# ScalarE's copy of a transposed tile, moved between the side work of two rounds in the fox stage

## What is computed

```python
s = einsum(q, k) * scale + fq[..., None] - cum_logf      # per block of 128 queries
s = where(k_pos <= q_pos, s, NEG_BIG)
p = softmax(s, axis=-1)
out = einsum(p, v)                                        # then a norm per head
# beside it in the same stage, from the other mixers:
y = gelu(y_s5); y = y * sigmoid(y @ w_glu)                # S5's gate
logf = log_sigmoid(z) + log1p(lb * exp(min(-z, 60)))      # HGRN2's gates
k = (1 - lb) * sigmoid(-z)
qk = silu(conv(concat(q, k)))                             # mLSTM's short convolution
```

## Time and profile before

| | us |
|---|---|
| median of 3 runs (1586.54 to 1592.84) | 1587.22 |
| the profiled execution | 1587.83 |
| its span, first to last instruction | 1586.0 |
| TensorE busy in it | 1505.0 (95%) |
| VectorE busy | 817.4 (52%) |
| ScalarE busy | 575.5 (36%) |
| GpSimd busy | 299.1 (19%) |
| the fox stage, 1009.86 to 1075.64 | 65.8 |

### The profile page before, as it was taken

How to read it: one execution, slowest core, us unless ns; L and a number is a source line. 1 busy time by engine, 2 the same in 40 slices (tenths; PEclk the granted TensorE clock), 3 DMA queues, 4 the chain that set the end, 5 groups by cost and what they waited for, 6 DMA issues and landing times. The chain is left out here.

```text
span 1586.0 us, 18617 instructions
## 1 busy us (share of the span) xinstructions
PE 1505.0 (95%) x7560; PEld 1227.5 (77%) x7560; DVE 817.4 (52%) x1137; ACT 575.5 (36%) x902; POOL 299.1 (19%) x298
## 2 busy tenths in 40 slices
PE   7999999989999999999998899898799999999997
PEld 5887887766788888888886677686678888888885
DVE  4232444478557447343437898577736443333425
ACT  4221544356636313132335322484225232112222
POOL 1000100000024894000003288325112000000000
PEclk9999999999999999999999999998799999999998
DMA  4322211310042223233232212110012233232222
GB/s 180 105 81 85 77 56 47 116 65 1 28 146 81 84 102 106 80 107 106 81 116 80 74 61 80 33 55 27 27 54 80 80 107 106 81 106 98 89 93 80
DMA packets 38859, 129.25 MB, mean 81 GB/s; under 512 B 4677, under 2 KB 23005, under 8 KB 27381
## 3 DMA queue, kind: packets, MB, share of 16 engines
q1 hardware_dynamic: 38484, 127.93, 23.6%
q10 hardware_dynamic: 288, 0.12, 0.0%
HBM read 124.82 MB, written 3.17 MB: 81 GB/s over the span
## 5 line engine op out<-in xcount | busy, mean ns | idle before, releaser
L242 PE MATMUL bank<-xT_hi,ring_hi 128*128 128x512 f32 (+3 forms) x920 | 356.6, 388 | 6.7 <-DVE xT_lo L1643 4.8
L223 DVE TENSOR_TENSOR ring_lo<-ring_raw,ring_hi 128x2048 fp32r<-128x2048 f32 (+2 forms) x113 | 260.6, 2309 | 184.2 <-ACT ring_hi L213 184.1
L242 PE MATMUL bank<-xT_lo,ring_hi 128*128 128x512 f32 (+3 forms) x920 | 352.9, 384 | 0.0
L242 PE MATMUL bank<-xT_hi,ring_lo 128*128 128x512 f32 (+3 forms) x920 | 352.6, 383 | 0.0
L213 ACT CAST ring_hi<-ring_raw 128x2048 fp32r<-128x2048 f32 (+3 forms) x115 | 212.9, 1852 | 244.2 <-DMA ring_raw<-in_w_ff 130.5
L242 PEld LDWEIGHTS bank<-xT_hi,ring_hi 128*128 128x128 f32 (+2 forms) x920 | 174.3, 189 | 49.0 <-issue 8.5
L242 PEld LDWEIGHTS bank<-xT_hi,ring_lo 128*128 128x128 f32 (+2 forms) x920 | 174.1, 189 | 34.2
L242 PEld LDWEIGHTS bank<-xT_lo,ring_hi 128*128 128x128 f32 (+2 forms) x920 | 174.4, 190 | 33.0
L242 PE MATMUL bank<-ring_hi,hid_hi 128*128 128x512 f32 x432 | 169.5, 392 | 3.8 <-DVE ring_lo L223 3.8
L242 PE MATMUL bank<-ring_hi,hid_lo 128*128 128x512 f32 x432 | 169.0, 391 | 0.0
L242 PE MATMUL bank<-ring_lo,hid_hi 128*128 128x512 f32 x432 | 169.0, 391 | 0.0
(11 more groups left out here) (496 smaller groups left out, 2145.7 us busy)
## 6 DMA issues: line engine op xcount, KB each, us to landing
ring_raw<-in_w_ff SPq DMA_DIRECT2D x30, 1024.0 KB, 4.8
ring_raw<-in_w_up SPq DMA_DIRECT2D x22, 1024.0 KB, 4.8
ring_raw<-in_w_proj SPq DMA_DIRECT2D x8, 1024.0 KB, 5.2
ring_raw<-in_w_gates SPq DMA_DIRECT2D x8, 1024.0 KB, 4.8
ring_raw<-in_w_fm SPq DMA_DIRECT2D x12, 512.0 KB, 5.0
ring_raw<-in_w_dn_a SPq DMA_DIRECT2D x6, 1024.0 KB, 4.9
ring_raw<-in_w_proj SPq DMA_DIRECT2D x8, 512.0 KB, 4.3
ring_raw<-in_w_out SPq DMA_DIRECT2D x4, 1024.0 KB, 4.9
```

What stands on the lines that cost most here:

```text
L223: k.nc.vector.tensor_tensor(k.ring.lo[:, g % SLOTS, 0:n], k.raw[:, g % SLOTS, 0:n], plain(k.ring.hi[:, g % SLOTS, 0:n]), ALU.subtract).the ...
L242: mm = k.nc.tensor.matmul(out, x, y, start=first and n == 0, stop=last and n == 3 * len(pairs) - 1)
```

## The change

ScalarE's copy of batch i's transposed tile moves from behind the side work of round i+1 to between that of round i and that of round i+1. TensorE's, VectorE's, GpSimd's and SyncE's lists stay as they are.

```diff
--- before.py
+++ after.py
@@ -1018,8 +1018,8 @@
                     exponentials(i + 1)
                 beside.act(act, i)
                 if i < nb:
+                    evac("act", act, i)
                     beside.act(act, i + 1)
-                    evac("act", act, i)
             if paired and not beside.early:
                 for r in range(nb + 1, beside.steps_on_pe + 1):
                     beside.act(act, r)
```

## The result

| | before | after |
|---|---|---|
| median of 17 runs each | 1590.48 us (1583.62 to 1592.96) | 1593.09 us (1591.44 to 1599.15) |
| ratio, with its 95% interval | | 1.0026 [1.0014, 1.0038] |
| the profiled execution | 1587.83 | 1592.79 |

A second comparison on another occasion (12 runs of the changed kernel, 35 of the kernel before) gave 1.0018 [1.0006, 1.0030]. The ratio is the measured one and not the quotient of the two medians, which is 1.0016; the means of the two comparisons differ by 4.1 and 2.7 us. The change makes the kernel slower, by about 3 to 4 us.

What follows compares the result with a forecast made beforehand. Waits, not a full engine, were taken to bound the fox stage. Terms +1.56 (pair 1), +0.6 (bank of tm 2) and +1.2 (pair 5, seen by pair 7) gave +3.4 us, 1590.6 from 1587.22; range 1587.6 to 1593.4.

Steps and rivals of the forecast that it cites:

- the third exponential: ScalarE, first pair: starts at 1021.8 instead of 1019.81, +2.0 us, behind the copy, two loads and the sigmoid.
- glu 1: TensorE work after ScalarE's copy of tile tm 1, pair 2: starts at 1032.65 instead of 1031.09, +1.56 us.
- The wait before tm 2: TensorE, pair 3: tile tm 2 waits for bank 6 until ScalarE's side activation ends at 1039.6; +0.6 us.
- the wait for pair 7's exponentials: TensorE, pair 7's transposes: held by exponentials delayed by pair 5's logarithm and load; +1.2 us, reaching +3.4.
- its transposes are ready 1.56 later too: Pair 3 on TensorE: transposes shift by 1.56 us, so the copy of 1035.62 runs at 1037.18 to 1037.66.
- pair 1's: First pair: sigmoid and its load fall behind the copy; +1.56 us on TensorE.
- C: Half-clock spells at glu 1 and next stage's head vanish, returning up to 1.8 and 1.5 us: 1587.3 to 1589.2; chance 0.10.
- D: New waits before tm 2 and pair 7's transposes lower the clock: +5.2 to +7.0 us, 1592.4 to 1594.2; chance 0.12.
- B: Second round's loads are issued before the copy, in its wait: not slower, end +0.4 us, 1587.6; chance 0.10.
- E: ScalarE stands after each load about another 1.28 us: end +6.0 us, 1593.2 (1593.4 by the skill's figure); chance 0.02.

## Why the prediction was right, and where it was not

**Bound and mechanism: right.** The waits decide, the moved copies themselves cost next to nothing (0.1 to 0.5 us in the stage), and the loads stand behind the copy. The prediction's rows do not show that an activation follows its load without a gap (both loads of the earlier trace rows have a wait for VectorE behind them), but the load and the sigmoid at 1018.05 and 1018.07 after do. Counted from the stage's start, the third exponential was forecast at 11.9 us and came at 11.98; glu 1 at 22.79 and came at 22.80. The wait before tm 2 (0.6 forecast, 0.44 in the trace) and the wait for pair 7's exponentials are there, and each pair alone gives its term: 1.55 (at glu 1), 0.6 and 1.05 (in the stage), against 1.56, 0.6 and 1.2.

**The sum in the stage: 3.4 forecast, 4.0 measured.** The failing step is that of pair 3, "its transposes are ready 1.56 later too". They were 1.9 later at their start and their end 2.2: in the changed kernel the lower clock lasted until 27.6 us of the stage, so that the mixing took 1.80 us and the transposes 1.10, against 1.07 to 1.43 and 0.83 in the five profiles of before, where it ended at 24.0 to 24.7. Over the same two us of the stage (25.5 to 27.5), before and after:

```profile
1035.36:1037.36 2.00, 2.00 (x13) 1.00 0.00 0
```

```profile
1033.96:1035.96 2.00, 2.00 (x11) 0.50 0.00 0
```

From there on everything is 0.6 later than forecast. The same late end, 27.5 to 28.0, is in all five profiles of kernels in which pair 1's loads stand behind its copy and no dummies are added; at 27.0 it also came in one of the two profiles with the five other pairs, so it is not pair 1's alone. I had priced the clock as rivals C and D, at other places and in whole spells; the case that came, a spell that ends a little later over the shifted work, was not among them. And a term of the sum holds for one state of the clock only: with the dummies pair 1's was gone.

**The time: 1590.6 forecast, 1593.1 measured.** The step that failed is the base, the median of three runs, 1587.2. Those were two of the lower group and one of the upper; with 17 runs the median is 1590.5. Against the median of 17, 1590.6 amounts to no change (+0.1), where the measured median is 2.6 higher. The prediction named the 6.3 us that the three runs span and then allowed only "the 1 us by which two medians of this kernel differ easily". In the ratio the forecast was 1.0021, which the intervals of both comparisons hold; that is in part luck, see below. The part behind the stage, which I took as unchanged, was 2.4 us longer than in the profiled execution before and 4.1 us shorter than in the upper group; over all 104 and 30 runs the means are 1590.3 and 1593.5, so +3.2. That this is near the forecast +3.4 is luck: the stage cost 0.5 to 1.0 more than forecast, by the profile of before that is taken, and the part behind it, weighted by the 44 and 60 runs of the two groups, came out about 1.4 us shorter than before, for which the prediction had no term. That 1593.1 lies within 1587.6 to 1593.4 is luck too, for the upper end stood there for rival D, whose spells did not come.

**The rivals.** B (loads ahead of the copy) did not happen by itself, but was made by hand, and its price of +0.4 came out at +0.2 to +0.5 (stage 65.97). Glu 1 came 0.31 later, where B had +0.3, but with the five other pairs' copies alone it was already 0.28 later (pair 2's copy then waits 0.19 us ahead of the logs, where the prediction had its bank ready), so that B's account of this term is not shown. C and D had the right kind of cause for what was missing, though at the wrong places: neither of the two spells was gone, none came at the new waits before tm 2 and the transposes of pair 7, and those at glu 1 and behind the stage grew. E, the drain after each load: ScalarE starts the sigmoid at 1018.07, the load before it ends at 1018.05. The rule of the Trainium skill, "ScalarE: Activation LUTs", section "What ACT_TABLE_LOAD costs", of a drain of about 1380 ns per switch, is not borne out here; the 1283 ns for the load are.

## What to carry to other kernels

Before moving an instruction that waits, list what falls behind it, and count the table loads: a load that lay in a wait can cost up to its full 1.28 us once a waiting instruction that needs no table stands in front of it, unless the engine has idle time behind it, and a one-column activation of the next function ahead of that instruction takes it back (stage 69.8 to 65.97 us here). Take the base from enough runs to see whether it has one group or two. Where it has two, read the granted clock window by window, and try dummy matmuls in TensorE's waits before anything finer: here they took about 4 us off the kernel before, and the cost of this order of the copies from 3.2 to 1.1 us.

## What was not expected of the hardware

The same program had two groups of times 5.5 us apart, and in its profiles TensorE ran at 1.2 GHz either for 3.5 or for 44 us after the same wait, with the stage ahead the same to 0.4 us. The clock also fell with TensorE busy without a gap, behind a stretch with many 64-column and one-column matmuls. What decides between the cases is left open; that the waits in front play a part is shown by the dummy matmuls, which left one group.
